# Odd mixer: score scale moved to the query copy, maxima negated in the reduction, cosine products of two rotations on GpSimd; context queries' second scores in the next PSUM bank

## The reference, cut to what matters

```
qa_c = _q_groups(aqc, qn_a, A_Q_HEADS, A_KV_HEADS, None)
o_ac = _flat(_attend(qa_c, ka_c, va_c, None))
```

```
a_bar = jnp.exp(lam * delta)
bu = jnp.einsum('bsgh,gph->bsgp', ug.astype(jnp.complex64), b_bar)
_, state = lax.associative_scan(s5_combine, (a_el, bu), axis=1)
...
scale = (MLA_NOPE + MLA_ROPE) ** -0.5
p = masked_softmax(sc * scale, chunk_causal_mask(start, s))
```

## Time and profile before

| | us |
|---|---|
| median of three runs | 2867.66 (2867.61 to 2867.77) |
| the profiled execution | 2863.03 |
| its span, first to last instruction | 2861.2 |
| TensorE busy in the span | 2773.6 |
| VectorE busy | 1369.0 |
| GpSimd busy | 1350.7 |
| ScalarE busy | 848.1 |

### The profile page before, as it was taken

One profiled execution on the slowest core, in us unless ns is written; L12 is line 12 of the kernel. 1 busy time (PEld: TensorE's weight loads), 2 busy tenths in 40 slices (PEclk: granted clock), 3 DMA queues, 4 the chain that ended last, 5 costly groups with the idle time before them and its releaser, 6 DMA issues.

```text
span 2861.2 us, 36702 instructions
## 1 busy us (share of the span) xinstructions
PE 2773.6 (97%) x14560; PEld 2166.2 (76%) x14560; DVE 1369.0 (48%) x2262; ACT 848.1 (30%) x1582; POOL 1350.7 (47%) x1106
## 2 busy tenths in 40 slices
PE   7999999999989999999999999999999999999997
PEld 5988777777878877677797666788787655788886
DVE  3412556666576222434944666524725956511113
ACT  3011432331130134322325354232233234222222
POOL 2445224224534754558765545744545313744433
PEclk9999999999999999999999999999999999999998
DMA  7111222222421122123322212232333311322322
GB/s 271 46 54 58 67 86 80 68 86 81 133 77 60 61 74 73 57 83 120 113 74 67 66 45 74 92 97 87 96 92 113 115 53 39 109 91 89 99 86 75
DMA packets 244836, 243.73 MB, mean 85 GB/s; under 512 B 5392, under 2 KB 234640, under 8 KB 244048
## 3 DMA queue, kind: packets, MB, share of 16 engines
q1 hardware_dynamic: 243376, 237.89, 26.3%
q0 software_dynamic: 1312, 3.80, 0.5%
HBM read 233.16 MB, written 7.34 MB: 84 GB/s over the span
## 4 chain that ended last, share of the span: by engine, by line
PE 87%; DVE 8%; ACT 2%; issue 1%; POOL 1%; SPq 1%; DMA 1%; DVEq 0%; POOLq 0%; ACTq 0%
PE psum L948 23%; PE psum L950 22%; PE psum L949 22%; PE psum L1211 4%; PE psum L1190 1%; PE psum L1146 1%; DVE columns L2679 1%; PE psum L1328 1%; PE psum L1166 1%; PE psum L1487 1%; PE psum L1145 1%; POOL columns L3398 1%; PE psum L1215 1%; PE psum L1507 1%; SPq L785 1%
## 5 line engine op out<-in xcount | busy, mean ns | idle before, releaser
L948 PE MATMUL psum<-columns,columns 128*128 128x512 f32 (+1 forms) x3464 | 1339.7, 387 | 16.0 <-POOL columns L3398 4.9
L950 PE MATMUL psum<-columns,columns 128*128 128x512 f32 (+1 forms) x3464 | 1261.7, 364 | 0.0
L949 PE MATMUL psum<-columns,columns 128*128 128x512 f32 (+1 forms) x3464 | 1260.2, 364 | 0.0
L3398 POOL TENSOR_TENSOR columns<-columns,columns 128x512 fp32r<-128x512 f32 (+1 forms) x676 | 905.3, 1369 | 436.8 <-ACT columns L1881 403.5
L3394 POOL TENSOR_TENSOR columns<-columns,columns 128x512 fp32r<-128x512 f32 x392 | 420.9, 1104 | 965.1 <-PE psum L950 761.3
L948 PEld LDWEIGHTS psum<-columns,columns 128*128 128x128 f32 x3464 | 653.9, 189 | 191.3 <-issue 68.5
L949 PEld LDWEIGHTS psum<-columns,columns 128*128 128x128 f32 x3464 | 654.3, 189 | 122.1 <-issue 25.9
L950 PEld LDWEIGHTS psum<-columns,columns 128*128 128x128 f32 x3464 | 652.9, 188 | 111.3
L1881 ACT ACTIVATE columns<-columns 128x1024 fp32r<-128x1024 f32 (+2 forms) x154 | 136.7, 935 | 172.5 <-PE psum L950 165.8
L2679 DVE SCALAR_TENSOR_TENSOR columns<-columns,columns,columns 128x256 f32<-128x256 f32 x224 | 153.7, 741 | 0.0
L2661 DVE SCALAR_TENSOR_TENSOR columns<-columns,psum 128x512 f32<-128x512 f32 x80 | 54.8, 685 | 188.2 <-PE psum L1211 183.3
(11 more groups left out here) (429 smaller groups left out, 2696.0 us busy)
## 6 DMA issues: line engine op xcount, KB each, us to landing
columns<-in_w_merge SPq DMA_DIRECT2D x32, 1024.0 KB, 6.8
columns<-in_w_ada SPq DMA_DIRECT2D x24, 1024.0 KB, 5.4
columns<-in_w_in SPq DMA_DIRECT2D x22, 1024.0 KB, 5.4
columns<-in_ev_w_in SPq DMA_DIRECT2D x22, 1024.0 KB, 5.3
columns<-in_ffn_gate SPq DMA_DIRECT2D x22, 1024.0 KB, 5.3
columns<-in_ffn_up SPq DMA_DIRECT2D x22, 1024.0 KB, 5.3
columns<-in_ffn_down SPq DMA_DIRECT2D x16, 768.0 KB, 4.8
columns<-in_ffn_down SPq DMA_DIRECT2D x16, 640.0 KB, 4.5
```

Of the source, the lines that this page charges most:

```text
L948: mm(dst, weights(0, k), moving(0, k), start=start and k == 0, stop=False)
L949: mm(dst, weights(0, k), moving(1, k), start=False, stop=False)
L950: last = mm(dst, weights(1, k), moving(0, k), start=False, stop=stop and k == k_tiles - 1)
L3398: last = g.tensor_tensor(low[:, c], raw[:, c], high[:, c].bitcast(F32), ALU.subtract)
```

## The change

Four things are changed. (a) In layer 0 the second head's scores of a context pair go into bank 5, and the wait between the two matmuls is gone. (b) In the odd mixer ScalarE multiplies the queries by 96^-0.5 when it copies them out of PSUM; the exponentials have no scale any more, and the maximum comes negated out of the reduction, so that L3282 is gone, 32 times. (c) The cosine products of `rot1` are made by GpSimd in place, when TensorE has read the tile, and VectorE subtracts from them. (d) Those of `rot2` are made by GpSimd too, right behind the scan and already shifted by one column, into `zz`; VectorE adds to them. A new semaphore `s5_cosines` counts the eight products.

```
 def score_columns(b, t, h):
     n_x = unit_keys(b, t)[1]
-    return (SCORES_AT + BANK - n_x if h < 2 else SCORES_AT + BANK + CTX), n_x + CTX
+    return SCORES_AT + BANK + (-n_x if h < 2 else CTX if n_x else BANK), n_x + CTX
...
-                        context_at = SCORES_AT + BANK + c * CTX
+                        context_at = SCORES_AT + BANK + c * (CTX if n_x else BANK)
...
                         scores(0, False).then_inc(scored, 1)
-                        pe.wait_ge(scored, base + u + 1)
                     scores(1, False).then_inc(scored, 1)
...
-                    f(pr_mla[0][:, u % 2, 0:n], psum[:, o:o + n], ACT.Exp, bias=cols[:, c:c + 1], scale=96 ** -0.5,
+                    f(pr_mla[0][:, u % 2, 0:n], psum[:, o:o + n], ACT.Exp, bias=cols[:, c:c + 1],
...
-                        f(qm[:, i, :], src, ACT.Copy).then_inc(side_freed["act"], 1)
+                        f(qm[:, i, :], src, ACT.Copy, scale=96 ** -0.5).then_inc(side_freed["act"], 1)
...
-                    order(v.tensor_reduce(c, s[:, 0:n], AX.X, ALU.max))
-                    v.tensor_scalar(c, c, -scale, None, ALU.mult).then_inc(maxed2, 1)
+                    v.tensor_reduce(c, s[:, 0:n], AX.X, ALU.max, negate=True).then_inc(maxed2, 1)
...
-                        if what == "rot1":
-                            order(tt(flat(zz)[:, c], flat(s_in)[:, c], flat(ct)[:, c], ALU.mult))
-                        else:
-                            order(tt(flat(s_in)[:, c], flat(s_in)[:, c], flat(ct)[:, c], ALU.mult))
                         tt(flat(z2)[:, c], src, flat(st)[:, c], ALU.mult).then_inc(side_freed["dve"], 1)
                         dve.wait_ge(side_freed["dve"], side_evicted(what, i))
+                        dve.wait_ge(s5_cosines, 4 * (what == "rot2") + i + 1)
                         if what == "rot1":
-                            order(tt(flat(zz)[:, c], flat(zz)[:, c], flat(z2)[:, c], ALU.subtract))
+                            order(tt(flat(zz)[:, c], flat(s_in)[:, c], flat(z2)[:, c], ALU.subtract))
                         else:
-                            order(tt(zz[:, g, 1:S5K], s_in[:, g, 0:S5K - 1], z2[:, g, 0:S5K - 1], ALU.add))
+                            order(tt(zz[:, g, 1:S5K], zz[:, g, 1:S5K], z2[:, g, 0:S5K - 1], ALU.add))
...
             pool.wait_ge(prepared, 12)
+            for i in range(4):
+                c = slice(8 * i, 8 * i + 8)
+                pool.wait_ge(odd_done, side_done("rot1", i))
+                g.tensor_tensor(s_in[:, c, :], s_in[:, c, :], ct[:, c, :], ALU.mult).then_inc(s5_cosines, 1)
             pool.wait_ge(side_freed["dve"], side_evicted("k7", 0))
             for j in range(S5J):
 
                 pool.dma_start(Tm[0:16 * (j + 1), j].rearrange("p g h -> p (g h)"), k7[16 * (7 - j):P, :]).then_inc(t_moved, 16)
+            pool.wait_ge(s5_rot_ready, 1)
+            for i in range(4):
+                c = slice(8 * i, 8 * i + 8)
+                g.tensor_tensor(zz[:, c, 1:S5K], s_in[:, c, 0:S5K - 1], ct[:, c, 0:S5K - 1], ALU.mult).then_inc(s5_cosines, 1)
```

More of the change, by code:

```diff
@@ L689, in build @@
         s5_rot_ready = sem("s5_rot_ready")
+        s5_cosines = sem("s5_cosines")
         t_moved = sem("t_moved")
@@ L3270, in odd_mixer @@
                 u0 = len(units)
-                scale = 96 ** -0.5
                 flat = lambda a: a.rearrange("p g k -> p (g k)")
```

## The result

The changed kernel takes 2850.36 us (median of five runs, 2849.57 to 2851.82), the kernel before in the same series 2867.61 (2862.57 to 2867.77). The ratio is 0.9948 with a 95% interval of 0.9936 to 0.9959, that is 14.9 us less (12 to 18). The forecast was 9.6 us less, 2858.1, and its range ended at 2854.5: the sign was right, the gain too small, and the time lies outside the range. The profiled execution took 2851.82 us with a span of 2850.0, 11.2 less than the span before.

The account below looks back on a forecast made before the run. TensorE, busy in 97% of the span, was taken as the bound, with VectorE's list the path in the odd mixer. Context pairs 6.4, negated maxima 0.33 and cosine products 2.9 made 9.6 us: 2858.1 from 2867.66, range 2854.5 to 2865.0.

Parts of the forecast that it names:

- a gain above 12 us: Whole run: all bounds at their good end and every negation counting; chance 0.03.
- three bounds: Range's lower end, 2854.5: context pairs 6.8, cosine products 3.8, and half of the negations' 5.4 us.
- the reading by lengths: Layer 0's context pairs: by record lengths a pair goes from 1.45 to 0.70 us, 0.75 less; 6.0 for eight.
- Both rivals on this term: Context pairs: halves don't overlap, only the hole goes, 3.7 us (chance 0.10); or nothing gained on TensorE (0.08).
- the three places: Behind the rotations, where the chain passes: one ahead of an exponential, two ahead of a weighting; 0.33 us together.
- Step one: rot1: with cosine products on GpSimd, the scan starts 0.9 us earlier, at 2343.9, and ends at 2348.3.
- its own rule: A VectorE instruction without a PSUM tile waits until the running GpSimd instruction ends, and no longer.
- Step three: rot2: GpSimd's shifted products run 2348.35 to 2353.4; unit 9's transposes start 0.5 us earlier, second swap ends 1.0 later.
- Step four: Swap's end to the memset: VectorE's 13.41 us lose 3.96, so the memset comes 2.9 us earlier, at 2363.55.
- Step two: The moved transfers' eight starts, 4.4 us from 2342.1, lie within the scan; GpSimd is free at 2346.5.
- The rival of a VectorE held until all four products are through: Odd mixer: GpSimd's run of four holds VectorE throughout; cosine part gives 0.7 us, run 2860.2; chance 0.14.
- the slower rival: GpSimd's product much longer than 1.27 us: 4.65 eats all other gains, 5.6 makes the run 5.7 us longer; chance 0.04.

Follow-up runs that it names:

- the run with filled holes: The kernel before, with unread 128x128 matmuls on TensorE, 8 ahead of the first gate job and 6 ahead of unit 23's transposes: 2860.31 us, ratio 0.9980.
- two versions of the changed kernel without a filler there: The changed kernel with rot1's products back on VectorE, 2850.19 us; the changed kernel with 18 unread matmuls in unit 9's hole, 2850.91 us.
- bank alone: The kernel before with the context queries' second scores in the next bank, but TensorE's wait between the two matmuls kept: 2865.24 us, ratio 0.9998.

## Why the prediction was wrong

**What failed: the end of the sum, "the rest of the program is TensorE's, and moves up as it is".** The sum counted lists and waits only. It had looked at the granted clock in one stretch, 2350.5 to 2355.2, and rightly found that VectorE covers it there: filled, it gave 0.05. The same look at the stretches behind would have shown 0.68 and 0.54 in places where TensorE's own matmuls are the path. They don't move up as they are: they had 3.8 us to lose or give, by the run with filled holes, and the trace of after has all of it (1.69 and, of 2.49, 2.12). Neither the sum nor a rival held this case: the chance of 0.03 for a gain above 12 us rested on path lengths, as did the range's lower end (whose three bounds add up to 13.3, a little more than the 13 that it allows). With 3.8 more the sum would have been 13.4, inside the measured 12 to 18. Of the 7.7 us between the time forecast and the time measured, 3.1 are the located parts (12.7 against 9.6), 2.4 the base, and 2.2 are located nowhere.

Why the clock stays up in after is shown for neither stretch by the hole's length alone. In the gate job the hole is 2.05 or 2.06 us in all traces without a filler there: after, its repeat and the cosine products alone at full clock, the nine others at half. In the last units the hole went from 1.79 to 1.42 us with the negated maxima, and in all five traces with them and without a filler there the units took 9.7 us; in the seven without either they took 11.3 to 12.2, and the filler alone brought 10.09. That speaks for the shorter hole as the cause, but it is a reading from traces that differ in other things too. What the gate job's clock hangs on stays open; it fell or held with edits elsewhere that leave its own hole as it was (cosine products alone: it held; negated maxima alone: it fell). So its 1.69 us can't be credited to the change: they are luck, as far as is known, in two profiled executions. In the two versions of the changed kernel without a filler there the gate job fell to half clock, and their medians (2850.19 and 2850.91) are no longer than 2850.36; which level the executions without a profile had is not known. The Trainium skill's page "TensorE: Matmul & The Clock Gate", section "What's actually happening", says that the point at which the clock changes isn't tied to the kernel and moves from run to run. That the gate job ran at either level behind one and the same hole fits that; but the two kernels that were profiled twice kept their level, and no run here shows the mechanism.

**The context pairs: right, 6.0 to 6.3 against 6.4.** The start to start is 0.63, not 0.53 to 0.58: eight times 0.75 is 6.0, the reading by lengths and the lower bound. Both rivals on this term fall: bank alone gives nothing, the pair without the wait overlaps, and no new wait took its place.

**Scale and negated maxima: 0.65 forecast, 1.0 measured on the path.** In the last units, at full clock in both, the kernel before with filled holes takes 10.09 and the negated one 9.73: 0.36, against 0.33 forecast for the three places. Up to the first output it gave 0.6 against 0.32. That the reduction negates for nothing is shown: it takes 0.29 us for 128 columns and 0.42 for 256, with the negation and without. What it gave beyond, 2.1 us in the last units, is the first point.

**The cosine products: 2.9 forecast up to the first output, with the negations there; 2.0 measured.** Step one failed. The scan should have started 0.9 earlier; it starts 0.14 later within the mixer (52.87 against 52.73 us). The forecast had the subtraction end at 2341.5 while GpSimd's fourth product ran until 2342.1, against its own rule that such an instruction waits until GpSimd's ends. The rule itself held: by it the subtraction would have ended 0.69 behind the fourth product, 1.3 later, and the term would have been some 1.6 us in place of 2.9 (an estimate from the forecast's own steps). In after the subtraction waited 0.73 for its product, began when the next one ran and ended at 2337.60, 0.55 behind that product's end (2334.49 + 2.56). The swap's last instruction ends 0.55 behind the last product too (2350.26 against 2349.71). The Trainium skill's page "GPSIMD Engine Reference", section "1. Specifications", lists the SBUF interfaces as shared with VectorE, with contention for VectorE instructions with two SBUF inputs; the trace agrees, with 1.74, 1.66 and 1.63 beside the products and 0.69 for the fourth subtraction, with none of the products beside it. PSUM readers kept 0.68.

Step three then has the swap end 2.2 later than before (63.27 against 61.03 us from the mixer's start) and not 1.0, mostly by the scan. Step four held: 9.45 us from there to the memset were forecast, 9.15 were measured. Step two held too: the transfers' starts were over at 2341.29 (2336.99 + 4.30), and GpSimd then waited 3.08 for the scan. Rot1's move shows no gain within the change: the first output is 0.3 later by it, and 0.2 later where it is alone; only beside rot2 without the negations, and counted from the matmul at 42.55, did it give 0.5 (30.80 with both, 31.29 with rot2's alone). The gain is rot2's and the negations' (2.3 by the run with just these two in the mixer). The rival of a VectorE held until all four products are through (0.7) falls: the weighting was held, 0.66 in place of 0.29, but ended 0.09 behind the first product (1.24), and readers of PSUM got through. GpSimd's product was never near the price of the slower rival.

**The base.** The median of three, 2867.66, lay about 2 us above the middle of the longer series. The forecast added the trace's gain to it, so that this error made the time forecast later, not the gain.

## What to carry to other kernels

Before summing list lengths, read the granted clock of every stretch in which TensorE's own matmuls are the path and which lies behind one of its holes: such a stretch can come out at the other level, by an edit next to it or by nothing that is known, and the two lengths of the same matmuls (here 3.51 and 5.20 us) are the two ends of a term that belongs in the range. A filler into the hole tells its price by itself. And of work given to GpSimd, count what VectorE is doing beside it: an instruction with two SBUF tiles of 128x512 cost about 1 us more there (1.63 to 1.74 for 0.69), so that products handed over gave nothing where a subtraction had to stand next to them.

## What was not expected of the hardware

- Fourteen matmuls that nobody reads made the kernel before 5.7 us faster (ratio 0.9980, 0.9971 to 0.9989), 3.8 of it in the trace, where TensorE stayed at 2.4 GHz behind places that were holes of 1.8 and 2.1 us.
- One and the same gate job behind one and the same hole of about 2.05 us ran at either level, 3.51 or 5.06 to 5.21 us, in traces whose lists around it are alike.
- VectorE's instruction with two SBUF inputs of 128x512 that stood beside a GpSimd product ended 0.54 to 0.55 us behind that product's end, four times in after: 1.27 to 1.74 us in place of 0.69.
